# A chain of two transformer blocks on one core: the first modulation as row products on TensorE, in slabs for quarters of the channels, and the first three weight slabs multiplied quarter by quarter

## The reference, cut to what matters

```python
c_act = jax.nn.silu(c)
mod = (c_act @ w_mod[l] + b_mod[l])[:, None, :]
shift_m, scale_m, gate_m, shift_f, scale_f, gate_f = jnp.split(mod, 6, axis=-1)
h = rms_norm(x, norm_mix[l]) * (1.0 + scale_m) + shift_m
z = h @ w_in[l]
```

## Time and profile before

| | |
|---|---|
| median of 3 runs | 2033.52 us |
| lowest and highest | 2031.78 and 2035.04 us |
| profiled execution | 2030.57 us |
| its span, first to last instruction | 2028.5 us |
| mean granted clock of TensorE | 0.99 |
| PE busy | 1980.4 us (98%) |
| DVE busy | 1702.0 us (84%) |
| ACT busy | 1257.4 us (62%) |

### The profile page before, as it was taken

One profiled execution on the slowest core, in us unless ns is written; L12 is line 12 of the kernel. 1 busy time (PEld: TensorE's weight loads), 2 busy tenths in 40 slices (PEclk: granted clock), 3 DMA queues, 4 the chain that ended last, 5 costly groups with the idle time before them and its releaser, 6 DMA issues.

```text
span 2028.5 us, 32745 instructions
## 1 busy us (share of the span) xinstructions
PE 1980.4 (98%) x13665; PEld 1771.3 (87%) x13665; DVE 1702.0 (84%) x1874; ACT 1257.4 (62%) x1269; POOL 39.5 (2%) x77
## 2 busy tenths in 40 slices
PE   7999999999999999999999999999999999999997
PEld 6889999999879899999878888888888888888886
DVE  6797888998786778887479898898988989898997
ACT  3469735654344554343367777777777777777775
POOL 3010000000000000000000000000000000000000
PEclk8999999999999999999999999999999999999999
DMA  9974876878643459999259999999999999999994
GB/s 310 302 248 138 264 235 224 263 235 277 219 165 105 146 194 332 320 322 324 84 208 368 368 354 371 350 374 361 362 361 355 369 352 370 367 354 369 368 372 158
DMA packets 337577, 589.16 MB, mean 290 GB/s; under 512 B 10518, under 2 KB 150316, under 8 KB 337425
## 3 DMA queue, kind: packets, MB, share of 16 engines
q1 hardware_dynamic: 333776, 580.70, 81.6%
q0 software_dynamic: 3008, 5.78, 1.0%
q10 hardware_dynamic: 640, 0.52, 0.1%
HBM read 585.89 MB, written 1.07 MB: 289 GB/s over the span
## 4 chain that ended last, share of the span: by engine, by line
PE 86%; DVE 8%; issue 3%; ACT 2%; DMA 1%; SPq 0%; DVEq 0%; ACTq 0%
PE bk L669 15%; PE bk L671 15%; PE bk L670 15%; PE bk L663 10%; PE bk L664 10%; PE bk L665 10%; DVE wlo L1969 2%; DVE macc L1994 2%; PE bk L1214 1%; ACT whi L1351 1%; DMA raw<-in_w_mod 1%; DVE uc L2349 1%; PE bk L1263 1%; PE bk L1126 1%; PE bk L725 1%
## 5 line engine op out<-in xcount | busy, mean ns | idle before, releaser
L1969 DVE TENSOR_TENSOR wlo<-raw,whi 128x2048 fp32r<-128x2048 f32 x477 | 1080.3, 2267 | 204.5 <-ACT whi L1351 203.2
L1351 ACT CAST whi<-raw 128x2048 fp32r<-128x2048 f32 x477 | 903.7, 1895 | 376.6 <-PE bk L671 249.0
L663 PE MATMUL bk<-HH,whi 128*128 128x256 f32 x1480 | 420.6, 284 | 0.9 <-DVE KC L2245 0.4
L664 PE MATMUL bk<-HL,whi 128*128 128x256 f32 x1480 | 410.4, 277 | 0.0
L665 PE MATMUL bk<-HH,wlo 128*128 128x256 f32 x1480 | 409.0, 276 | 0.0
L669 PE MATMUL bk<-whi,xh 128*128 128x512 f32 x896 | 354.4, 396 | 0.0
L671 PE MATMUL bk<-wlo,xh 128*128 128x512 f32 x896 | 349.3, 390 | 0.0
L670 PE MATMUL bk<-whi,xl 128*128 128x512 f32 x896 | 349.0, 390 | 0.0
L663 PEld LDWEIGHTS bk<-HH,whi 128*128 128x128 f32 x1480 | 276.9, 187 | 6.6 <-issue 3.8
L664 PEld LDWEIGHTS bk<-HL,whi 128*128 128x128 f32 x1480 | 279.6, 189 | 1.1 <-issue 0.7
L665 PEld LDWEIGHTS bk<-HH,wlo 128*128 128x128 f32 x1480 | 276.9, 187 | 0.0
(11 more groups left out here) (378 smaller groups left out, 2465.2 us busy)
## 6 DMA issues: line engine op xcount, KB each, us to landing
raw<-in_moe_w SPq DMA_DIRECT2D x334, 1024.0 KB, 6.5
raw<-in_ada_w SPq DMA_DIRECT2D x56, 1024.0 KB, 5.6
raw<-in_ff_w SPq DMA_DIRECT2D x40, 1024.0 KB, 5.9
raw<-in_w_in SPq DMA_DIRECT2D x29, 1024.0 KB, 5.5
raw<-in_w_mod SPq DMA_DIRECT2D x24, 1024.0 KB, 5.7
raw<-in_w_up SPq DMA_DIRECT2D x22, 1024.0 KB, 5.1
raw<-in_attn_w_qkv SPq DMA_DIRECT2D x12, 1024.0 KB, 5.6
raw<-in_w_branch SPq DMA_DIRECT2D x8, 1024.0 KB, 5.2
```

The source lines that it names most:

```text
L663: pe.matmul(o, sh, mh, start=start, stop=False, skip_group_check=True)
L664: pe.matmul(o, sh, ml, start=False, stop=False, skip_group_check=True)
L1351: act.copy(halves_at(q, g)[0], raw[q.slot[i]][:, :n]).then_inc(q.hi_done.mark(g), 1)
L1969: dve.tensor_tensor(low, raw[q.slot[i]][:, :n], high.bitcast(F), ALU.subtract).then_inc(q.taken.mark(i), 1)
```

## The change

The first modulation no longer goes through DVE's sums. Each quarter q of the channels (256 of them) has two slabs of kind "D": w = 0 for the scale, w = 1 for the shift, each 8 chunks by 256 columns. `c32` holds each chunk of c in 32 equal columns. `pe_rows` makes eight products with c32 as stationary and the slab as moving operand, chunk k in the 32 partitions from 32 (k mod 4) on; ACT copies the bank to `rowsum`, and `pe_rows_turn` turns it to columns and sums the four groups of partitions with `pick` (1 at partitions 0, 32, 64, 96). DVE adds the two halves and the bias.

The three first slabs of w_in are interleaved with the quarters, and `pe_mixer` multiplies them in parts, as the channels come. "kv" and the first "qc" change places. The dummy products ahead of z0 are gone; x is loaded ahead of all slabs.

```diff
-        zjob = [("qa", 0, 0), ("qa", 1, 256), ("kv", 0, 512), ("qc", 0, 2816), ("qc", 1, 3072), ("kc", 0, 3328),
+        zjob = [("qa", 0, 0), ("qa", 1, 256), ("qc", 0, 2816), ("kv", 0, 512), ("qc", 1, 3072), ("kc", 0, 3328),
...
-        first = [s for g in (2, 3, 0, 1) for s in mslabs(wmod, g, 0)]
-        st_order = first + order[0:3]
+        quarter = [[("D", (q, w), gslabs(wmod, 8, c0 + 256 * q, None)[0][2], 8, 256) for w, c0 in enumerate((D, 0))] for q in range(4)]
+        st_order = quarter[0] + order[0:1] + quarter[1] + order[1:2] + quarter[2] + order[2:3] + quarter[3]
...
-        early = (6, 7, 8, 0, 1, 2, 3, 6, 8)
+        early = (6, 7, 0, 8, 6, 1, 7, 8, 2, 6, 7)
...
-        def pe_mod_direct(ring, g):
...
+        def pe_rows(q, w):
+
+            u = take(Z_T, "row", q, w)
+            i = st.direct[q, w]
+            v = raw[st.slot[i]][:, :].rearrange("p (k n) -> p k n", k=8)
+            if q == 0 and w == 0:
+                pe.wait_ge(*(yield from dve_step.of("c32")))
+            pe.wait_ge(st.raw_in[st.slot[i]], 16 * st.use[i])
+            for k in range(8):
+                r, half = 32 * (k % 4), k // 4
+                t = pe.matmul(u.t[r:r + 32, half * S:(half + 1) * S], c32[:, k, :], v[:, k, :], start=True, stop=True, skip_group_check=True)
+            t.then_inc(st.summed.mark(i), 1)
...
+        def pe_rows_turn(q, w):
+
+            u = take(Z_T, "first", q, w)
+            pe.wait_ge(*(yield from N.of("row", q, w)))
+            for half in range(2):
+                for j in range(2):
+                    for r in range(0, 128, 32):
+                        c = half * S + j * 128 + r
+                        t = pe.matmul(u.t[r:r + 32, 2 * half + j:2 * half + j + 1], rowsum[w][:, c:c + 32], pick[:, 0:1],
+                                      start=True, stop=True, skip_group_check=True)
+            t.then_inc(u.fill(), 1)
...
-                if t == 0:
-                    spare(u.t[:, 0:128], 14)
...
+            for q, between, behind in ((1, ((0, 0, 2),), ((0, 2, 4),)), (2, ((1, 0, 4),), ((0, 4, 6), (1, 4, 6))),
+                                       (3, (), ((2, 0, 6), (0, 6, 8), (1, 6, 8), (2, 6, 8)))):
+                yield from pe_rows(q, 0)
+                yield from pe_rows_turn(q, 0)
+                for what in between:
+                    yield from part(*what)
+                yield from pe_rows(q, 1)
+                yield from pe_rows_turn(q, 1)
+                for what in behind:
+                    yield from part(*what)
             yield from pe_z_side(1)
+            yield from pe_z_side(2)
...
+            for q in range(4):
+                for w in range(2):
+                    if q:
+                        act.wait_ge(*(yield from B.full("first", q - 1, w)))
+                    act.wait_ge(*(yield from B.full("row", q, w)))
+                    u = B.at["row", q, w]
+                    act.copy(rowsum[w][:, :], u.t[:, :]).then_inc(u.sem, 1)
+                    N.note(("row", q, w), u.drained())
+                    if q == 0 and w == 0:
+                        yield from act_stat("x0")
+                act.wait_ge(*(yield from N.of("coeff", q, 1)))
+                for c in (2 * q, 2 * q + 1):
+                    act.wait_ge(*(yield from dve_step.of("t", "h0", c)))
+                    act.activation(HH[:, c, :], sqb[q % 3][:, c % 2 * S:c % 2 * S + S], AF.Identity,
+                                   bias=modT[0][:, c:c + 1]).then_inc(xhi_done.mark("h0", c), 1)
+                if q < 3:
+                    yield from act_hi(st, q)
...
+            for q in range(4):
+                if q:
+                    yield from dve_lo(st, q - 1)
+                yield from summed(q, 0)
...
+                for c in (2 * q, 2 * q + 1):
+                    yield from scaled(c)
+                yield from summed(q, 1)
+                for c in (2 * q, 2 * q + 1):
+                    yield from low(c)
```

More of the change, by code:

```diff
@@ L402, in build @@
             st_order += at_slot.get(t - NP, [])
-        early = (6, 7, 8, 0, 1, 2, 3, 6, 8)
+        early = (6, 7, 0, 8, 6, 1, 7, 8, 2, 6, 7)
         for i, entry in enumerate(st_order):
[L405 to L409, removed]
+            st.add(entry, early[i] if i < 11 else (i - 8) % NR)
+            if entry[0] == "D":
+                st.direct[entry[1]] = i
         order = st_order
@@ L441, in build @@
             s_ = i % (NR + NX)
[L442 to L448, removed]
+            st.add(entry, (s_ + first_moe - 8) % NR if s_ < NR else s_)
+        mlist = [(which, g, when) for (which, g), _, when in mplan]
         last_slab = {(t[0], t[1]): i for i, (kind, t, *_) in enumerate(st.plan) if kind == "M" and t[2] == 1}
@@ L547, in sp_main @@
                 sp.dma_start(xn[:, tb, :], a["x"][0, tb * 128:(tb + 1) * 128, :]).then_inc(arrived, 16)
-            yield from sp_weights(st, 2, len(st.plan))
+            yield from sp_weights(st, 0, len(st.plan))
         def pool_main():
@@ L802, in pe_start @@
                     yield from pe_stats(Z_S, "x0", c - 4)
+            u = take(Z_T, "vec", 0)
+            pe.wait_ge(*(yield from N.of("vn", 0)))
+            pe.transpose(u.t[:, 0:128], vn[0][:, :], ident).then_inc(u.fill(), 1)
+            yield from pe_rows(0, 0)
             yield from pe_stats(Z_S, "x0", 4)
             yield from pe_stats(Z_S, "x0", 6)
[L805 to L808, removed]
+            yield from pe_rows_turn(0, 0)
+            yield from pe_rows(0, 1)
+            yield from pe_rows_turn(0, 1)
         def pe_scores(h):
@@ L1412, in act_start @@
             act.preload_act_table_set("natural_log_exp_and_others")
[L1413 to L1416, removed]
             for c in range(0, 8, 2):
@@ L1423, in act_start @@
             act.wait_ge(*(yield from dve_step.of("eps")))
[L1424 to L1436, removed]
+            act.wait_ge(*(yield from B.full("vec", 0)))
+            u = B.at["vec", 0]
+            act.copy(vt[0][:, :], u.t[:, 0:128]).then_inc(u.sem, 1)
+            N.note(("vec", 0), u.drained())
+            for q in range(4):
[15 more added lines that the diff above has]
+                    yield from act_hi(st, q)
         def act_head(h, step):
@@ L2083, in dve_start @@
[L2083 to L2094, removed]
+            dve.memset(pick[:, :], 0.0).then_inc(dve_step.mark("pick0"), 1)
@@ new lines, in dve_start @@
+            dve.wait_ge(*dve_step.now())
+            for r in range(0, 128, 32):
+                dve.memset(pick[r:r + 1, :], 1.0).then_inc(dve_step.mark("pick"), 1)
+            dve.wait_ge(*(yield from N.of("cst")))
+            dve.wait_ge(*(yield from N.of("csil")))
+            for k in range(8):
+                dve.tensor_scalar(c32[:, k, :], one[:, 0:32], csil[:, k:k + 1], None, ALU.mult).then_inc(dve_step.mark("c32"), 1)
+            scaled, low = modulation("h0", X, HH, HL, 0, 0, 0, sqb)
@@ new lines, in summed @@
+            def summed(q, w):
+                c = 8 * (1 - w) + 2 * q
+                dve.wait_ge(*(yield from B.full("first", q, w)))
+                u, o = B.at["first", q, w], modT[0][:, c:c + 2]
+                dve.tensor_tensor(o, u.t[:, 0:2], vec("b_mod")[:, c:c + 2], ALU.add).then_inc(dve_step.mark("first"), 1)
+                dve.wait_ge(*dve_step.now())
+                dve.tensor_tensor(o, u.t[:, 2:4], o, ALU.add).then_inc(u.sem, 1)
+                dve.wait_ge(*u.drained())
+                N.note(("coeff", q, w), u.drained())
```

56 lines of the change are left out of this document (21 added, 35 removed).

## The result

| | before | changed |
|---|---|---|
| median of 14 runs each | 2032.24 us (2029.56 to 2035.81) | 2037.85 us (2035.95 to 2039.99) |
| profiled execution, its span | 2030.57, 2028.5 us | 2037.54, 2036.1 us |

The ratio is 1.0028, with a 95% interval from 1.0021 to 1.0035: the change makes the kernel 5.6 us slower. The profiled executions lie 7.0 us apart; that of before was 1.7 us under its median of 14 and that of the changed kernel 0.3 under, and 7.0 - 1.7 + 0.3 is 5.6.

The account below looks back on a forecast made before the run. PE, busy 98% of the span, bounds the kernel, so only its start can be won. Fourth slab at 73.5 us, plus 5 for the clock, minus 73.3 gives +5.2 on the median 2033.52: 2039 us, range 2029 to 2049.

Parts of the forecast that it names:

- The mark: End of the fourth slab, read by ACT at 73.30 us before; its shift was taken as the gain or loss.
- Row products: Eight fp32 products on four column tiles per slab (pe_rows): tiles run side by side, 1.05 us with the tail.
- Rival 2: Slower still: four column tiles take turns (+11 us) or the clock stays low throughout (+25); 2045 to 2060 us, chance 0.15.
- The chain at full clock: Quarters' row products, copies, turnings, casts and k-steps in series, PE at full clock: z0 complete at 54.0 us.
- the sum: The prediction's step-by-step addition of times: 73.5 at full clock, plus 5 for the clock, minus 73.3, gives +5.2 us.
- signs of being wrong: Row products of 3 us, clock 1.00 from 25 us, chain waiting for data, or PE idle time later making up the lag.
- The new wait: Before "kv", now fourth and writing bank 1: PE stands 3.5 us until DVE normalizes z0, 11.0 us after z0's end.
- The clock: PE's short pieces and waits between 20 and 75 us: two or three falls to 0.50 on the chain, 5 us.
- Edits costed at nothing: Among them DVE's six slab sums removed: they ran under the transfers, so freeing an idle engine gives nothing.
- Rival 3: Quarters two to four paced by the landings, not the chain: gain of 4 to 9 us, 2025 to 2029.5, chance 0.14.
- Rival 1: The clock holds, none or one fall: 2034 to 2036 us, no change; chance 0.26 together with rival 4.
- rival 4: The change does nothing because data come too late anyway: Rival 1's times, chance 0.26 together with it.

Follow-up runs that it names:

- e3_both: Changed kernel with "kv" in a bank of ring 3, 4 and unread dummy products in PE's waits, none ahead of "kv": 2027.10 us, 0.9977 of the kernel before.
- e1_bank: Changed kernel with one edit, "kv" writing a bank of the ring 3, 4 instead of bank 1: 2032.96 us, 1.0003 of the kernel before.
- e4_swap: Kernel before with one edit, "kv" and the first "qc" exchanged in the list of slabs: 2030.76 us, 0.9996 of the kernel before.
- e2_fill: Changed kernel with 128-column products that nobody reads in the places where PE would wait: 2031.58 us, 0.9998 of the kernel before.
- e5_acc: Changed kernel with chunks 4 to 7 added in PSUM to chunks 0 to 3, so copy and turning halve: 2033.98 us, 1.0012 of the kernel before.

## Why the prediction was right

The forecast of 2039.0 us lies 1.2 over the measured 2037.85, and the two causes that it named, the wait for bank 1 and the low clock, are the ones that the runs show. That the number came so close is in part luck. The mark was forecast 5.2 us late and is 8.0 late; the medians came out 5.6 apart. Of the 2.4 us between, 0.5 was made up inside the kernel, 0.6 lies around the span, and 1.4 is how the two profiled executions happen to lie against their medians.

- *The mark as measure of the gain.* Right: +8.0 at the mark, +7.56 near the end. In the experiments the differences of the marks and of the medians, both against the kernel before, agree within 3 us, which is as much as some of the effects; the marks stand against one execution of before that was 1.7 us under its median, which is part of that.
- *Row products.* Right: 1.05 us forecast, 1.07 measured at full clock and 1.93 at the low one. The four column tiles run side by side; 16 passes in turn would be 3.8 us by the forecast's 0.24 us a pass. Rival 2's first half falls, and so does its second, since the clock is 1.00 from 38.07 to 68.79. The Trainium skill ("TensorE: Matmul & The Clock Gate", Part 3, packing small matmuls) has 2.38 times for three column tiles (512 columns). Here four tiles gain more than the page has for three: by estimate 3.8 / 1.07, some 3.6 times. Passes of the same kind on the whole array follow each other at 0.215 us in the kernel before (two from 19.27 to 19.70), and sixteen of those in turn would be 3.4 us; in e3_both, where the next product starts at once, the eight row products take 1.00 us (45.26 to 46.26). By this second estimate it is 3.4 times.
- *The chain at full clock.* Nearly right. Forecast for z1's first product was 34.2 and for z0's end 54.0. In e3_both, at clock 1.00 and with its dummy products in line, z0 is squared at 55.48. From z1's first product to the fourth quarter's first row product the sum had 9.6 us (34.2 to 43.8); the changed kernel has 10.0 (39.13 to 49.11), and from there to z0's end 10.2 against 10.4. So the later half was sized rightly, and of the 4.9 us by which z1's first product came late all but 0.5 arose behind 25.27, where z0's first product stands (24.8 in the sum), most of it by the low clock: in e3_both these two products are at 25.18 and 35.37. The sum also had the data too early. PE takes up the second quarter's first slab at 21.96 us, having waited for it, where 3.0 us a megabyte from 7.5 on gives 19.5; this wait was in no term, and a chain that waits for data was among the prediction's signs of being wrong. For this one slab the sign came true, but it moved z0's first product by no more than the 0.5 us above.
- *The new wait.* Right in place, releaser and size: 3.5 us forecast, 3.28 measured, with 10.5 us from z0's end (59.5 to 70.0) for 11.0. e1_bank shows it to be worth 4.4 us of the mark, and e4_swap that the exchange alone doesn't bring it about.
- *The clock.* Right in kind, somewhat under-sized: 5 us forecast, 5.9 us shown by e2_fill. The picture behind the number was off: it wasn't two or three falls of 3.4 us but one stretch of 17.07, under which the second quarter and the start of the third lie, and one of 6.83. Nor does every fall cost half its length, as the sum took from the one at 506.37 (see the last section). This term and the chain make the mark's 8.0: 5.9 for the clock, 2.1 for the rest, of which the sum had 0.2.
- *Edits costed at nothing.* DVE's freed sums brought nothing visible, though no run takes them apart, and between the quarters PE waited for data once only, for 3.55 us. Rival 3 (faster, paced by the landings) falls: the chain comes to its last quarter at 49.11, and PE waits for no slab there. Rival 1 (the clock holds) falls by the windows, and rival 4 with it, since the time did change.

What I hadn't weighed is how near the idea was to a gain. Its two side effects are worth 10 us together (e3_both against the changed kernel), and either could be removed in a line or a few.

## What to carry to other kernels

When slabs change places, look up which result bank each now writes and what frees that bank, not only whether its data are there: here an exchange that is free by itself cost 4 us once the work ahead of it ended later. Read the granted clock under a chain of small steps as well as its waits: here it ran at 0.50 for 17 us, and dummy products in the waits won 6 us. A change that does several things at once should be cut into its parts before it is given up: the interleaving gained, and two side effects ate it.

## What the runs showed of the hardware

- Four column tiles of 32, each with its own moving operand of 256 columns in fp32, run side by side: eight products, 16 records, in 1.07 us. Adding the second four into the same columns (e5_acc) works as well.
- A busy PE doesn't always have the full clock. In the earlier trace rows it is busy 17.07 of 17.07 us at 0.50, for the first 11.6 of them under the direct group's products of one column (to 36.68), and the clock is back 5.0 us after the 128-column dummy products begin; in e2_fill it is busy 17.88 of 18.00 us at 1.00, with the row products, slab products and 128-column dummy products.
- Not every fall costs. The kernel before has the clock at 0.50 at 506.37. The same work lies some 8.3 us later in the changed kernel, and there the clock is 1.00:

```profile
502.00:530.00 28.00, 25.89 (x249) 25.50 (x247) 22.56 (x31) 11.55 (x11) 0.00 (x0) 1.00 0.85 282
```

Yet the changed kernel gains nothing by it. The same step on ACT ahead of that fall and behind it, first in the kernel before and then in the changed one, is 8.31 us apart both times:

```profile
503.31 0.90 ACT L1393 ACTIVATE HHc<-uc,mod_c 128x256 fp32r<-128x256 f32 x2
511.51 0.91 ACT L1393 ACTIVATE HHc<-uc,mod_c 128x256 fp32r<-128x256 f32 x2 [4.14 <-DVE uc L2033]
```

```profile
511.62 0.90 ACT L1415 ACTIVATE HHc<-uc,mod_c 128x256 fp32r<-128x256 f32 x2
519.82 0.91 ACT L1415 ACTIVATE HHc<-uc,mod_c 128x256 fp32r<-128x256 f32 x2 [4.13 <-DVE uc L2059]
```

The sum had counted this fall at 1.7 us. DVE is busy 3.34 of 3.41 us in it and 3.38 of 3.42 behind it, and ACT waits for DVE in the rows above, so here DVE and not PE seems to set the time; that is argued, not tested. The kernel before falls twice more, near 974 and 1035 us, where the changed kernel doesn't: over both together its lag goes from 7.77 to 7.68 us. So look which engine sets the time under a fall before you price it by its length.
